# In the second block's weight stream, GpSimd instead of VectorE subtracts the rounded half of each tile

## The chip, the cores and the metric

The kernel runs on one core of one Trainium2 chip. The metric is the device time of one execution in microseconds (us), the median of several runs. Engines are named as the profile names them: PE is TensorE (PEld its weight loads), DVE is VectorE, ACT is ScalarE, POOL is GpSimd, SP is SyncE, whose queue issues nearly all DMAs.

## What is computed

Two transformer blocks run one after the other over 512 tokens of width 1024, all in fp32. The first block (four mixers, a gated merge, 32 experts) isn't touched by the change. The second block has two layers with these steps:

```python
h = rmsnorm(x, norm_pre[l])
(hq, hf_f, hf_b, hi, hz, ca, cb, cz, sb, sc, sv, sz,
 aq, ak, av, az, mq, mz) = split_cols(h @ w_in[l])
y_hg = hgrn2_branch(...)            # gated scan, forward and backward
y_cf = conformer_branch(...)        # depthwise convolution of 31 taps
y_sc = short_conv_branch(...)
y_at = window_attention(...) * jax.nn.silu(az)
mem_kv = rmsnorm(mem, mem_norm[l]) @ w_mem_kv[l]
y_mem = memory_cross_attention(mq, mem_kv) * jax.nn.silu(mz)
for n, yb in enumerate((y_hg, y_cf, y_sc, y_at, y_mem)):
    term = jax.nn.sigmoid(h @ w_gate[l, n]) * (yb @ w_branch[l, n])
    merged = term if merged is None else merged + term
x = x + rmsnorm(merged @ w_out[l], norm_post[l])
```

## The kernel before

**Split products.** A large product `W^T x` is made from rounded and residual halves in the format fp32r: `w_hi` is the tile rounded by ACT, `w_lo = w - w_hi` the rest, and the activations are kept as `x_hi` and `x_lo`. PE adds `w_hi*x_hi + w_hi*x_lo + w_lo*x_hi`, for each of eight slices of the contraction: 24 matmuls of 512 columns for one tile of 128 output channels (256 columns in `memory_keys`).

**The stream.** All weight tiles of a layer of the second block go through one `Stream`: 74 tiles a layer, 34 of projections (`w_in`) and 40 of the gates, and 8 tiles for both layers together in `memory_keys`, which runs once before the layers. That is 156 tiles in an execution. Raw tiles come in pairs into three slots `raw`; `w_hi` and `w_lo` have two buffers each. For tile n:

- ACT (`round`, L2053) waits until the raw pair is there and until PE has finished tile n-2 (`acc_done`), casts raw to `w_hi[n % 2]` and raises `rounded`.
- DVE (`rest`, L2077) waits for `rounded`, subtracts `w_hi` from raw into `w_lo[n % 2]` and raises `split`.
- PE (`pe`, L2111 to L2113) waits for `split` and runs the 24 matmuls into `acc[n % 2]`.
- ACT (`evict`, L2060 or L2064) copies `acc` out, or takes a tanh of it into `sg` where the tile is a gate.
- For a gate tile PE also runs two fp32 matmuls of the branch output (L2123, into `br`), after the previous gate tile's `mixed`, and DVE (`mix`, L2088 and L2094) multiplies them with `sg` and adds them to `merged`.
- SP (`load`) waits for `split` of the last tile of a raw slot before it loads the next pair into it.

Rounding and subtraction run one tile ahead of PE: `act` and `dve` of step n handle tile n+1, and evict or mix tile n-1.

**What sets the order.** Each engine has its program written out by hand, one stage after another; a stage is a block with a barrier at its end, and POOL begins every stage by clearing the semaphores of the one before (L171). Each layer has five stages that hold steps of the stream, and between the steps DVE does the stage's own work: `window_stage` (21 subtractions), `memory_stage` (8), `hgrn_stage` (12), `conv_stage` (18) and `merge_stage` (15). In `hgrn_stage` DVE computes scan arguments, scaled keys, masks and states in a written order with a stream step after each. In `conv_stage` the 31 taps of two channel tiles are 62 DVE instructions (L2797, L2799), five to a step, each of which adds `pad * w` to `conf`, the name `y_t` in the trace. DVE's `Chain` makes it wait for each of its own results.

```python
for s, n in enumerate(fill):
    stream.dve(dve, n)
    if s == 0:
        dve.wait_ge(blank, 2)
        dve.wait_ge(th_ready, 1)
        run(nc.vector.scalar_tensor_tensor(pad[:, :, H:H + S], th[:], 1.0, ca, ALU.add, ALU.mult))
    for tap in range(PER * s, min(PER * s + PER, 2 * TAPS)):
...
            run(nc.vector.scalar_tensor_tensor(conf[:, m, :], src, wt, conf[:, m, :], ALU.mult, ALU.add))
```

Of the kernel before, what the change touches and what calls it, by code (L numbers as in the profile page):

```python
# [15 lines left out]
F32 = mybir.dt.float32  # L16
# [1966 lines left out]
class Stream:  # L1983
# [87 lines left out]
        if n:  # L2071
            self.evict(act, n - 1)

    def rest(self, dve, n):
        if n < len(self.tiles):
            dve.wait_ge(self.rounded, n + 1)
            self.nc.vector.tensor_tensor(self.w_lo[:, n % 2], self.weights(n), self.w_hi[:, n % 2].bitcast(F32),  # L2077
                                         ALU.subtract).then_inc(self.split, 1)

    def mix(self, dve, n):  # L2080
# [11 lines left out]
        else:  # L2092
            dve.wait_ge(self.added, u)
            self.nc.vector.tensor_tensor(dst, dst, sg, ALU.add).then_inc(self.added, 1)  # L2094

    def dve(self, dve, n):
        if n == 0:
            self.rest(dve, 0)
        self.rest(dve, n + 1)
        if n:  # L2100
            self.mix(dve, n - 1)

# [153 lines left out]
def window_stage(c, stream, lead, fill, wj, k2, v, sink, y, strips):  # L2256
# [7 lines left out]
    with ExitStack() as ctx:  # L2264
# [4 lines left out]
        with c.stage() as block:  # L2269
            @block.sync  # L2270
            def _(sp):
# [9 lines left out]
                for s in range(steps):  # L2281
                    att.load_bias(sp, s + 2)
                    if s < len(fill):
                        stream.load(sp, fill[s] + 2)

            @block.tensor
            def _(pe):
                for n in lead:
                    stream.pe(pe, n)
                    if n == lead[3]:  # L2290
                        pe.wait_ge(stream.freed, lead[1] + 1)
                        for i in range(NT):
                            mm = pe.transpose(att.tps[:, 0, i * P:(i + 1) * P], vt[:, i * P:(i + 1) * P], c.const("ident"))
                        mm.then_inc(v_turned, 1)
                pe.wait_ge(k2_in, 64)
                pe.wait_ge(v_ready, 1)
                pe.wait_ge(stream.freed, lead[3] + 1)
                att.scores(pe, 0)
                for s in range(steps):
                    att.pe_step(pe, s)  # L2300
                    if s < len(fill):
                        stream.pe(pe, fill[s])
# [31 lines left out]
def memory_stage(c, stream, fill, qm, km, vm, y):  # L2334

    nc = c.nc
    gate = qm[:, 2:4]
    units = head_units(qm[:, 0:2], lambda h, b: km[b:b + 64, h // 2], lambda h, j: vm[:, j, h * HD:(h + 1) * HD],
                       y, 4, lambda i: (0, 2), None)
    with ExitStack() as ctx:  # L2340
        att = Attention(c, ctx, units, HD ** -0.5, gate)
        th = c.sb(ctx, "tanh", [P, 2, S])
        th_ready = c.sem("th")
        steps = len(units) + 2

        def beside(s):
            return [fill[s // 2]] if s % 2 == 0 and s // 2 < len(fill) else []

        with c.stage() as block:
            @block.sync  # L2350
            def _(sp):
                for n in fill:
                    stream.load(sp, n + 2)

            @block.tensor
            def _(pe):
                att.scores(pe, 0)
                for s in range(steps):
                    att.pe_step(pe, s)
                    for n in beside(s):  # L2360
                        stream.pe(pe, n)

            @block.scalar
            def _(act):
                nc.scalar.activation(th[:], gate, ACT.Tanh, scale=0.5).then_inc(th_ready, 1)
                for s in range(steps):
                    att.exps(act, s)
                    for n in beside(s):
                        stream.act(act, n)
                    att.turned(act, s - 1)  # L2370

            @block.vector
            def _(dve):
                att.run = Chain(dve, att.chain)
                for s in range(steps):
                    if s == 2:
                        dve.wait_ge(th_ready, 1)
                        att.run(nc.vector.scalar_tensor_tensor(gate, th[:], 1.0, gate, ALU.add, ALU.mult))
                    att.dve_step(dve, s)
                    for n in beside(s):  # L2380
                        stream.dve(dve, n)
# [73 lines left out]
def hgrn_stage(c, stream, fill, room, gate, lb, gain, y):  # L2455
# [6 lines left out]
    with ExitStack() as ctx:  # L2462
# [25 lines left out]
        with c.stage() as block:  # L2488
            @block.sync
            def _(sp):  # L2490
                for n in fill:
                    stream.load(sp, n + 2)

            @block.tensor
            def _(pe):
# [221 lines left out]
def conv_stage(c, stream, fill, glu, rest, w31, w3, bias, gain, shift, conf, short):  # L2717
# [6 lines left out]
    with ExitStack() as ctx:  # L2724
# [7 lines left out]
        with c.stage() as block:  # L2732
# [5 lines left out]
            @block.gpsimd  # L2738
            def _(pool):
                nc.gpsimd.memset(pad[:], 0.0).then_inc(blank, 1)  # L2740
                nc.gpsimd.memset(pad3[:], 0.0).then_inc(blank, 1)

            @block.tensor
            def _(pe):
# [116 lines left out]
def merge_stage(c, stream, fill):  # L2861

    with c.stage() as block:
        @block.sync
        def _(sp):
            for n in fill:
                stream.load(sp, n + 2)

        @block.tensor
        def _(pe):  # L2870
            for n in fill:
                stream.pe(pe, n)

        @block.scalar
        def _(act):
            for n in fill:
                stream.act(act, n)
            stream.evict(act, fill[-1])

        @block.vector  # L2880
        def _(dve):
            for n in fill:
                stream.dve(dve, n)
            stream.mix(dve, fill[-1])
# [244 lines left out]
```

## Time and profile before

| | |
|---|---|
| median of 3 runs | 3080.27 us (3079.12 to 3086.88) |
| the profiled execution, its own time | 3078.07 us |
| its span in the trace | 3076.3 us |
| PE busy | 2415.0 us, 79% |
| DVE busy | 1304.4 us, 42% |
| ACT busy | 739.3 us, 24% |
| POOL busy | 90.8 us, 3% |
| DMA queue of SP | 28.8% of 16 engines |
| mean granted TensorE clock | 0.85 |

The profile is one execution. Its span is 1.8 us shorter than that execution's time and its time 2.2 us under the median. "Idle before" is the time an engine stood before a group's instructions, with the instruction that released it. The second block runs from about 1608 us to the end: `memory_keys` to 1682 us, the first layer's stream from 1711 to 2298 us, the second's from 2407 to 2992 us. PE's records are pipelined: a matmul of 512 columns is shown with 0.39 us but the next starts 0.227 us later.

### The profile page before, as it was taken

What the parts mean: (1) busy time and instruction counts of PE and PEld (TensorE: products, weight loads), DVE (VectorE), ACT (ScalarE), POOL (GpSimd) and SP (SyncE); (2) the same over time, 40 slices, a digit from 0 to 9 for tenths busy, and PEclk for the clock granted to TensorE, in tenths of its full rate; (3) what the DMA queues carried; (4) which work ended last, traced back from release to release, by engine and by line L of the source; (5) the groups of instructions that cost most, each with busy time, mean ns of one, the idle gap of its engine ahead of it and who ended that gap; (6) DMA issues with size and microseconds to landing.
All of it is one profiled execution on the core that took longest, in us unless ns stands there. A gap on an engine that the chain in (4) does not pass through costs nothing. (4 is left out here: it accounts for less than half of the span.)

```text
span 3076.3 us, 30601 instructions
## 1 busy us (share of the span) xinstructions
PE 2415.0 (79%) x11062; PEld 1704.0 (55%) x11062; DVE 1304.4 (42%) x2309; ACT 739.3 (24%) x1285; POOL 90.8 (3%) x144
## 2 busy tenths in 40 slices
PE   5966457466998619999914799999985799999996
PEld 3833235355776514444404676677764676677764
DVE  1126843723333411111143345668533344668533
ACT  2222222201222101111103333322222333323221
POOL 0000000000000011111100000000000000000000
PEclk7965567556999759999966899999997899999997
DMA  4110100002221048777623432123311432123311
GB/s 151 36 71 22 31 30 20 11 7 104 102 102 55 16 118 302 267 265 266 224 97 111 125 109 49 52 69 100 117 55 60 132 102 65 52 69 96 115 53 73
DMA packets 264772, 300.05 MB, mean 98 GB/s; under 512 B 53667, under 2 KB 225779, under 8 KB 264630
## 3 DMA queue, kind: packets, MB, share of 16 engines
q1 hardware_dynamic: 255158, 289.78, 28.8%
q0 software_dynamic: 9472, 8.43, 0.8%
q8 instruction: 83, 1.36, 0.2%
q14 instruction: 59, 0.48, 0.1%
HBM read 289.13 MB, written 33.14 MB: 105 GB/s over the span
## 5 line engine op out<-in xcount | busy, mean ns | idle before, releaser
L2111 PE MATMUL acc<-x_hi,w_hi 128*128 128x512 f32 x1184 | 492.2, 416 | 16.5 <-DVE w_lo L2077 13.2
L2112 PE MATMUL acc<-x_lo,w_hi 128*128 128x512 f32 x1184 | 466.0, 394 | 0.0
L2113 PE MATMUL acc<-x_hi,w_lo 128*128 128x512 f32 x1184 | 465.9, 394 | 0.0
L2077 DVE TENSOR_TENSOR w_lo<-raw,w_hi 128x1024 fp32r<-128x1024 f32 x156 | 190.6, 1223 | 257.4 <-ACT w_hi L2053 254.3
L2053 ACT CAST w_hi<-raw 128x1024 fp32r<-128x1024 f32 x156 | 162.6, 1044 | 568.1 <-PE acc L2113 535.3
L2111 PEld LDWEIGHTS acc<-x_hi,w_hi 128*128 128x128 f32 x1184 | 225.9, 191 | 76.4 <-issue 18.2
L2112 PEld LDWEIGHTS acc<-x_lo,w_hi 128*128 128x128 f32 x1184 | 225.9, 191 | 54.7 <-issue 10.6
L1785 PE MATMUL ps<-wgu,xt 128*128 128x512 f32 x512 | 230.5, 603 | 30.6 <-ACT xt L1808 23.9
L2113 PEld LDWEIGHTS acc<-x_hi,w_lo 128*128 128x128 f32 x1184 | 225.1, 190 | 49.2
L1785 PEld LDWEIGHTS ps<-wgu,xt 128*128 128x128 f32 x512 | 95.6, 192 | 146.7 <-issue 118.4
L2123 PE MATMUL br<-y_t,raw_b 128*128 128x512 f32 x320 | 153.9, 604 | 7.2 <-DVE sg L2088 7.2
L1842 DVE TENSOR_TENSOR hid<-silu,ps 128x256 f32<-128x256 f32 x32 | 13.5, 421 | 273.2 <-ACT silu L1815 273.2
L1229 PE MATMUL ps<-x_hi,w_hi 128*128 128x512 f32 x256 | 113.9, 445 | 16.1 <-DVE w_lo L1290 16.1
L1775 PE MATMUL ps<-wd,hid_t 128*128 128x512 f32 x256 | 115.2, 593 | 0.9 <-DVE hid_t L1847 0.9
L360 PE MATMUL acc<-x_hi,w_hi 128*128 128x512 f32 x216 | 86.0, 398 | 25.8 <-DVE w_lo L349 25.8
L1328 PE MATMUL ps<-w_hi,m_hi 128*128 128x512 f32 x192 | 77.9, 405 | 34.5 <-DVE w_lo L1344 34.5
L1231 PE MATMUL ps<-x_hi,w_lo 128*128 128x512 f32 x256 | 100.9, 394 | 0.0
L1230 PE MATMUL ps<-x_lo,w_hi 128*128 128x512 f32 x256 | 100.5, 393 | 0.0
L2799 DVE SCALAR_TENSOR_TENSOR y_t<-pad,w,y_t 128x512 f32<-128x512 f32 x120 | 90.1, 751 | 3.4
L2123 PEld LDWEIGHTS br<-y_t,raw_b 128*128 128x128 f32 x320 | 60.7, 191 | 54.3 <-issue 48.3
L361 PE MATMUL acc<-x_lo,w_hi 128*128 128x512 f32 x216 | 85.3, 395 | 0.0
L362 PE MATMUL acc<-x_hi,w_lo 128*128 128x512 f32 x216 | 85.2, 395 | 0.0
(513 smaller groups left out, 3541.0 us busy)
## 6 DMA issues: line engine op xcount, KB each, us to landing
raw<-in_w_gate SPq DMA_DIRECT2D x40, 1024.0 KB, 5.2
raw<-in_w_in SPq DMA_DIRECT2D x34, 1024.0 KB, 5.5
wgu<-in_moe_w_gate SPq DMA_DIRECT2D x32, 1024.0 KB, 5.6
wgu<-in_moe_w_up SPq DMA_DIRECT2D x32, 1024.0 KB, 9.6
wd<-in_moe_w_down SPq DMA_DIRECT2D x32, 1024.0 KB, 11.5
wg<-in_w_in SPq DMA_DIRECT2D x8, 2048.0 KB, 7.7
y_t<-in_w_out SPq DMA_DIRECT2D x6, 2048.0 KB, 7.8
raw_b<-in_w_branch SPq DMA_DIRECT2D x40, 256.0 KB, 2.7
```

Source lines behind the costliest of these rows:

```text
L1229: pe.matmul(ps[:, m, :], hi, x_hi[:, k, :], start=(k == 0), stop=False)
L1230: pe.matmul(ps[:, m, :], hi, x_lo[:, k, :], start=False, stop=False)
L1231: pe.matmul(ps[:, m, :], lo, x_hi[:, k, :], start=False, stop=(k == KT - 1))
L1775: mm = pe.matmul(ps[:, 1 + 2 * u + half, :], ht[:, u, m * P:(m + 1) * P], wd[:, s % 4, m, half * 512:half * 512 + 512], start=(m == 0), st ...
L1785: mm = pe.matmul(ps[:, 0, :], xt[:, u, k, :], wgu[:, s, k, :], start=(k == 0), stop=(k == KT - 1))
L2053: self.nc.scalar.copy(self.w_hi[:, n % 2], self.weights(n)).then_inc(self.rounded, 1)
L2077: self.nc.vector.tensor_tensor(self.w_lo[:, n % 2], self.weights(n), self.w_hi[:, n % 2].bitcast(F32), ALU.subtract).then_inc(self.split, 1)
L2111: pe.matmul(acc, hi, tile.hi[:, k, :], start=(k == 0), stop=False)
L2112: pe.matmul(acc, hi, tile.lo[:, k, :], start=False, stop=False)
L2113: mm = pe.matmul(acc, lo, tile.hi[:, k, :], start=False, stop=(k == KT - 1))
L2123: mm = pe.matmul(self.br[:], self.raw_b[:, b % self.SLOTS, k, tile.half * P:(tile.half + 1) * P], tile.row[:, k, :], start=(k == 0), stop= ...
L2799: run(nc.vector.scalar_tensor_tensor(conf[:, m, :], src, wt, conf[:, m, :], ALU.mult, ALU.add))
```

## The change

The subtraction `rest` is issued by GpSimd instead of VectorE, with the same wait and the same semaphore. A new method `pool` issues it, one tile ahead as before, and every stage that holds stream steps gets a GpSimd program that does nothing else. In `conv_stage` it comes behind two memsets that GpSimd has there already. Nothing is changed for PE, ACT and SP.

```diff
-    def rest(self, dve, n):
+    def rest(self, pool, n):
         if n < len(self.tiles):
-            dve.wait_ge(self.rounded, n + 1)
-            self.nc.vector.tensor_tensor(self.w_lo[:, n % 2], self.weights(n), self.w_hi[:, n % 2].bitcast(F32),
+            pool.wait_ge(self.rounded, n + 1)
+            self.nc.gpsimd.tensor_tensor(self.w_lo[:, n % 2], self.weights(n), self.w_hi[:, n % 2].bitcast(F32),
                                          ALU.subtract).then_inc(self.split, 1)
...
+    def pool(self, pool, n):
+        if n == 0:
+            self.rest(pool, 0)
+        self.rest(pool, n + 1)
+
     def dve(self, dve, n):
-        if n == 0:
-            self.rest(dve, 0)
-        self.rest(dve, n + 1)
         if n:
             self.mix(dve, n - 1)
...
             def _(pool):
                 nc.gpsimd.memset(pad[:], 0.0).then_inc(blank, 1)
                 nc.gpsimd.memset(pad3[:], 0.0).then_inc(blank, 1)
+                for n in fill:
+                    stream.pool(pool, n)
```

The other four stages get a GpSimd program of the same loop (`for n in [*lead, *fill]` in `window_stage`, `for n in fill` elsewhere).

Below is POOL's order from the semaphore clears before `hgrn_stage` to `merge_stage`, the change against the kernel before. `ISA` at L171 is a clear of one semaphore, a branch enters a stage's program, and lines after L2077 have moved down by the inserted ones.

```order
 L171 ISA x13
+L2506 UNCONDITIONAL_BRANCH
+L2077 TENSOR_TENSOR w_lo<-raw,w_hi 128x1024 x12
 L167 UNCONDITIONAL_BRANCH
 L168 UNCONDITIONAL_BRANCH
 L171 ISA x27
-L2738 UNCONDITIONAL_BRANCH
-L2740 MEMSET pad 128x1084
-L2741 MEMSET pad_676 128x1028
+L2755 UNCONDITIONAL_BRANCH
+L2757 MEMSET pad 128x1084
+L2758 MEMSET pad_676 128x1028
+L2077 TENSOR_TENSOR w_lo<-raw,w_hi 128x1024 x18
```

POOL has nothing in `hgrn_stage` before, and 12 subtractions now; in `conv_stage` 18 subtractions stand behind the 27 clears and the two memsets.

DVE in `hgrn_stage`, before, from the subtraction behind `states(0)` to `scaled(1)`, whose products PE transposes next:

```order
L2077 TENSOR_TENSOR w_lo<-raw,w_hi 128x1024
L2088 SCALAR_TENSOR_TENSOR sg<-sg,br 128x512
L2094 TENSOR_TENSOR merged<-merged,sg 128x512
L2612 TENSOR_TENSOR_SCAN cum<-consts,g 128x512 x2
...
L2624 TENSOR_TENSOR ke<-end,cum 128x1024
L2077 TENSOR_TENSOR w_lo<-raw,w_hi 128x1024
L2088 SCALAR_TENSOR_TENSOR sg<-sg,br 128x512
L2094 TENSOR_TENSOR merged<-merged,sg 128x512
L2667 COPY y_t<-ps 128x4x64 x4
L2669 TENSOR_TENSOR y_t<-y_t,ps 128x2x448
L2630 TENSOR_TENSOR ke<-room,ke 128x1024
```

and the same stretch in the change:

```order
L2088 SCALAR_TENSOR_TENSOR sg<-sg,br 128x512
L2094 TENSOR_TENSOR merged<-merged,sg 128x512
L2629 SCALAR_TENSOR_TENSOR cum<-consts,g 128x512 x2
...
L2641 TENSOR_TENSOR ke<-end,cum 128x1024
L2088 SCALAR_TENSOR_TENSOR sg<-sg,br 128x512
L2094 TENSOR_TENSOR merged<-merged,sg 128x512
L2684 COPY y_t<-ps 128x4x64 x4
L2686 TENSOR_TENSOR y_t<-y_t,ps 128x2x448
L2647 TENSOR_TENSOR ke<-room,ke 128x1024
```

Two subtractions are gone from in front of `ke`; the rest stands as it stood.

DVE in `conv_stage`, before, in the middle of the taps:

```order
L2799 SCALAR_TENSOR_TENSOR y_t<-pad,w_551,y_t 128x512 x5
L2077 TENSOR_TENSOR w_lo<-raw,w_hi 128x1024
L2799 SCALAR_TENSOR_TENSOR y_t<-pad,w_551,y_t 128x512 x5
L2802 SCALAR_TENSOR_TENSOR rest<-tanh,rest 128x1024
L2077 TENSOR_TENSOR w_lo<-raw,w_hi 128x1024
```

and in the change, where the taps follow each other with nothing between:

```order
L2816 TENSOR_SCALAR y_t<-pad,w_551,conf_b 128x512 x2
L2818 SCALAR_TENSOR_TENSOR y_t<-pad,w_551,y_t 128x512 x33
```

## Rows read from the trace of the kernel before

**Rows 1.** Waits of PE, 1705 to 2300 us (first layer): total us, times, longest us.
```profile
PE acc L2111 <- DVE w_lo L2077: 6.9, 1, 6.9
PE br L2123 <- DVE sg L2088: 4.4, 2, 3.8
PE t_ps L2171 <- DVE probs_n L2219: 2.9, 7, 0.7
PE ps L2502 <- DVE ke L2630: 2.9, 1, 2.9
...
PE ps L2512 <- DVE rel L2633: 0.8, 1, 0.8
```

**Rows 2.** The same, 2405 to 3000 us (second layer).
```profile
PE br L2123 <- DVE sg L2088: 2.8, 2, 2.2
...
PE ps L2512 <- DVE rel L2633: 2.0, 2, 1.2
```

**Rows 3.** The page's costliest groups: busy us, mean ns, idle before, releaser.
```profile
L2077 DVE TENSOR_TENSOR w_lo<-raw,w_hi 128x1024 fp32r<-128x1024 f32 x156 | 190.6, 1223 | 257.4 <-ACT w_hi L2053 254.3
L2053 ACT CAST w_hi<-raw 128x1024 fp32r<-128x1024 f32 x156 | 162.6, 1044 | 568.1 <-PE acc L2113 535.3
```

**Rows 4.** Timeline, one tile of window_stage: start us, us, engine, line, operation.
```profile
1722.14 1.05 ACT L2053 CAST w_hi<-raw 128x1024 fp32r<-128x1024 f32 x1 [8.60 <-PE acc L2113]
...
1723.22 1.23 DVE L2077 TENSOR_TENSOR w_lo<-raw,w_hi 128x1024 fp32r<-128x1024 f32 x1 [8.24 <-ACT w_hi L2053]
...
1727.32 0.39 PE L2111 MATMUL acc<-x_hi,w_hi 128*128 128x512 f32 x1
```

**Rows 5.** Timeline, one tile of memory_keys.
```profile
1663.77 1.23 DVE L2077 TENSOR_TENSOR w_lo<-raw,w_hi 128x1024 fp32r<-128x1024 f32 x1 [1.66 <-ACT w_hi L2053]
...
1665.32 0.28 PE L2111 MATMUL acc<-mem_hi,w_hi 128*128 128x256 f32 x1
```

**Rows 6.** Groups of POOL: its smallest instruction that reads SBUF.
```profile
L1715 POOL COPY gi<-table 128x1 uint32 (+1 forms) x32 | 6.4, 199 | 24.5 <-PE ps L1765 16.3 <-DVE xg L1825 8.2
```

**Rows 7.** Timeline, hgrn_stage, DVE and then ACT.
```profile
1955.01 1.23 DVE L2677 TENSOR_SCALAR room<-g 128x2048 f32<-128x2048 f32 x1
...
1987.14 1.23 DVE L2077 TENSOR_TENSOR w_lo<-raw,w_hi 128x1024 fp32r<-128x1024 f32 x1
...
1998.43 1.23 DVE L2077 TENSOR_TENSOR w_lo<-raw,w_hi 128x1024 fp32r<-128x1024 f32 x1
...
2003.96 1.23 DVE L2630 TENSOR_TENSOR ke<-room,ke 128x1024 f32<-128x1024 f32 x1
...
1989.61 1.04 ACT L2053 CAST w_hi<-raw 128x1024 fp32r<-128x1024 f32 x1 [8.48 <-PE acc L2113]
...
2002.43 1.03 ACT L2053 CAST w_hi<-raw 128x1024 fp32r<-128x1024 f32 x1
```

**Rows 8.** Timeline, conv_stage, POOL, DVE and then PE.
```profile
2066.40 0.95 POOL L2741 MEMSET pad<- 128x1028 f32 x1
...
2067.80 1.23 DVE L2791 SCALAR_TENSOR_TENSOR pad<-tanh,glu 128x1024 f32<-128x1024 f32 x1 [1.64 <-ACT tanh L2761]
...
2094.15 3.90 DVE L2799 SCALAR_TENSOR_TENSOR y_t<-pad,w,y_t 128x512 f32<-128x512 f32 x5
...
2126.41 0.68 DVE L2088 SCALAR_TENSOR_TENSOR sg<-sg,br 128x512 f32<-128x512 f32 x1
...
2069.47 0.39 PE L2111 MATMUL acc<-x_hi,w_hi 128*128 128x512 f32 x1
...
2131.08 1.88 PE L2123 MATMUL br<-y_t,raw_b 128*128 128x512 f32 x4
```

**Rows 9.** Windows, a tile behind a stage change and the next: us, busy, PEclk, DMA.
```profile
1860.80:1868.60 7.80, 7.80 (x26) 6.13 (x25) 4.69 (x10) 2.62 (x6) 0.00 (x0) 0.68 0.54 4
1873.10:1878.50 5.40, 5.40 (x26) 4.49 (x27) 3.67 (x9) 2.28 (x5) 0.00 (x0) 1.00 0.37 127
```

More of the change, by code:

```diff
@@ L2284, in _ @@
                         stream.load(sp, fill[s] + 2)
+            @block.gpsimd
+            def _(pool):
+                for n in [*lead, *fill]:
+                    stream.pool(pool, n)
             @block.tensor
@@ L2353, in _ @@
                     stream.load(sp, n + 2)
+            @block.gpsimd
+            def _(pool):
+                for n in fill:
+                    stream.pool(pool, n)
             @block.tensor
@@ L2492, in _ @@
                     stream.load(sp, n + 2)
+            @block.gpsimd
+            def _(pool):
+                for n in fill:
+                    stream.pool(pool, n)
             @block.tensor
@@ L2741, in _ @@
                 nc.gpsimd.memset(pad3[:], 0.0).then_inc(blank, 1)
+                for n in fill:
+                    stream.pool(pool, n)
             @block.tensor
@@ L2867, in _ @@
                 stream.load(sp, n + 2)
+        @block.gpsimd
+        def _(pool):
+            for n in fill:
+                stream.pool(pool, n)
         @block.tensor
```

## Prediction

> **What bounds the kernel now.** I read the waits of PE first. In the first layer's stream of some 590 us PE waits for DVE in few places [rows 1]: 6.9 us for the layer's first `w_lo`, 4.4 us in two waits of the branch product for `sg`, 2.9 us for `ke`, 0.8 us for `rel`, and seven times 0.4 us for `probs_n` in `memory_stage`, a chain of small instructions with no subtraction ahead of it. The second layer shows `sg` and `rel` with 2.8 and 2.0 us [rows 2] and the row for `ke` again, word for word. These three, 8.1 and 7.7 us, lie in `hgrn_stage`. Everywhere else PE has work, so the stream is bound by PE, and a DVE that gets lighter helps in `hgrn_stage` alone.
>
> Then the groups. DVE spends 190.6 us on 156 subtractions of 1.22 us [rows 3]; this is what leaves DVE. ACT stood 535 of its 568 us of idle time before `w_hi` because PE had not finished the tile two back, not for a DMA. So the raw tiles come early, and loads that SP issues one us later (it waits for `split`) stay hidden under that margin.
>
> Then one tile of the steady stream [rows 4]. The cast ends at 1723.19 us, DVE subtracts to 1724.45, PE takes the tile at 1727.32: 2.87 us to spare, so a subtraction of up to 4.1 us costs PE nothing here. PE's time for a tile is 24 times 0.227, 5.44 us. In `memory_keys`, with 256 columns, the margin is 1665.32 - 1665.00 = 0.32 us [rows 5].
>
> **The price of one subtraction on POOL.** The trace has no two-input instruction on POOL. Below: its memset of 1028 columns takes 0.95 us, and it reads nothing [rows 8]. Above: two reads and a write in turn, three such passes, plus the 0.2 us of a POOL copy of one element [rows 6], 3.05 us. Two passes with the write beside them and the 0.2 give 2.1 us. I take X = 2.3 us, nearer to two passes than to three; both ends stay for the range.
>
> The Trainium skill, GPSIMD Engine Reference, section 3.1 (elementwise), gives 4497 ns for a two-input add over 2048 fp32 columns, as an estimate 2.25 us for 1024. No row here shows it. By it the sum would be some 2 us lower.
>
> **The change part by part.**
> - *First tiles.* The first tile of `memory_keys` and of each layer is waited for in full [rows 1]. Three times X - 1.22 = 1.08: **+3.2 us**.
> - *memory_keys.* Tiles 2 to 7 have 0.32 us to spare: six times 1.08 - 0.32 = 0.76: **+4.5 us**.
> - *Start of `conv_stage`.* POOL clears 27 semaphores and does two memsets before its first subtraction, which can start at 2067.35 [rows 8] and ends at 2069.65. PE wants that tile at 2069.47: 0.2 us late, **+0.4 us** for both layers. Other stages begin with 4 to 17 clears, hidden behind the cast and the tile made ahead.
> - *All other tiles.* X is under 4.1 us: nothing. PE covers it; the cost beyond it would be X - 4.1 a tile.
> - *`hgrn_stage`, DVE's side.* The first `sg` wait has one subtraction of 1.14 us (start to start) right ahead of it; the second `sg` wait, `ke` and `rel` have two (at 1987.14 and 1998.43, with `ke` from 2003.96) [rows 7]; the second layer's first `rel` wait another 0.8. With nothing in exchange: 1.2 + 2.4 in the first layer, 1.2 + 0.8 + 2.4 in the second, **-8.0 us**.
> - *Everything else that DVE sheds* (taps, attention, merges) lies beside a busy PE: nothing.
>
> Without any effect of the two engines on each other this is +8.1 - 8.0, nothing.
>
> **What the two engines do to each other** is the unknown that decides. DVE passes 2048 columns of one input (`room<-g`) in 1.23 us [rows 7], and the subtraction reads two inputs of 1024 columns in the same 1.23: both draw 2048 columns. So DVE seems to have two read streams and the two-input instruction needs both, while POOL now reads two tiles of its own. Either POOL has a path of its own (price 0) or it takes one of DVE's (price up to X for each subtraction that meets a two-input DVE instruction). No row shows a large read of POOL beside DVE. I take the second end, since no row shows a third stream.
>
> The Trainium skill, SBUF — State Buffer, section "Who interferes with whom", says that DVE and GpSimd share a port pair under an exclusive lock, that a DVE instruction with two SBUF inputs contends with a GpSimd instruction that reads SBUF, and that the later one blocks until the other ends. By this rule the change loses; by ports of their own it breaks even. The trace neither confirms nor denies it.
>
> - *`conv_stage` with the price.* A tile's step on DVE is five taps, 3.9 us [rows 8]. With a subtraction of its own, 1.14 from start to start, it is 5.04 us, under PE's 5.44. With X of standing still it is 6.2 us: **DVE becomes the bound.** PE needs the first `mix`, behind 55 taps, at 2131.08 for its branch product; before it was there at 2127.1. Now from 2067.80: two 1024-column instructions 2 x 1.4, 55 taps of 0.78 = 42.9, the mix 0.7, that is 2114.2; the first subtraction of POOL holds DVE X - 0.45, eleven more hold it X each: 2113.75 + 12 X. Against 2131.08 PE waits 12 X - 17.3 = 10.3 us. Point of break-even: X = 1.44 us. Behind such a stand PE's clock is lower for a while: behind a stage change the granted clock was 0.68, between its levels 1.2 and 2.4 GHz, and 26 matmuls took 7.8 where they take 5.4 us at 1.00 [rows 9]; I put 2 us. **+24.6 us** for two layers.
> - *`hgrn_stage` with the price.* Casts end at 1990.65 and 2003.46 [rows 7], inside DVE's run of two-input instructions in front of `ke` and `rel`; one more does so in the first half. Three holds of X against four subtractions of 1.14: 3 X - 4.6 = 2.3 us a layer, **+4.6 us** in place of -8.0.
>
> **Sum:** 3.2 + 4.5 + 0.4 + 24.6 + 4.6 = 37.3 us on the profiled execution's 3078.07: 3115.4. That execution lies 2.2 us under the median of the three runs, so I forecast **3118 us**. With X = 1.9 the same sum is 3100, with 2.75 it is 3138, with 3.05 about 3150; with 0.95 it is under 3078.
>
> **Rivals.**
> - *No interference (not slower).* DVE's taps stay at 0.78 us apart and POOL works beside them. Place: `conv_stage` and `hgrn_stage`. For it: the two engines have instruction streams of their own and PE hides a slower subtraction; against: the count of read streams. 3078.07 + 8.1 - 8.0 + 2.2 = **3080 us**, 3076 with X = 1.9 and 3088 with 3.05. It decides once a two-input DVE instruction beside POOL lasts as long as alone. Chance 0.35.
> - *Partial interference.* DVE loses a part of X, up to half, under the break-even of 1.44 us: only the 8 us of small terms and a little in `hgrn_stage`. Around 3085 to 3100. Chance 0.09.
> - *POOL too slow.* X over 4.1 us: PE waits on most of the 156 tiles, each X - 4.1, and at 5 us that is beyond 3180. Three passes are 3.05, so it needs a conversion to fp32r at a cost that no row shows. Chance 0.04.
> - That POOL is the one that gets held (it loses to DVE's next tap each time) is no case of its own: taps and subtraction still add up to 6.2 us a tile.
>
> **How the numbers follow.** Forecast 0.52, rivals 0.35, 0.09 and 0.04. A measurement of this kernel can tell about 0.3%, 9 us, from no change: under 3071 is faster, over 3089.5 slower. Slower: 0.52 + 0.04 + 0.06 = 0.62. Same: 0.33, nearly all of it the first rival. Faster 0.05: no case that I worked out gets there, only one with X near 1 us and gains in clock. The likeliest case's own range is 3100 to 3138; as the first rival must be let in, the range is 3077 to 3138, which leaves out the lowest tail of that rival and X over 2.75.
>
> **What would show it.** POOL's group L2077: 156 times, mean about 2.3 us, POOL busy near 450 us where it was 91. DVE's taps (now L2818): instructions of 0.75 us beside POOL either stay or reach up to 3 us, or start late with POOL as the reason; the group's mean or the idle time before it would grow by some 25 us a layer. PE's wait for `sg` in `conv_stage` about 10 us once a layer, the taps' end near 84 instead of 70 us after their start. In `memory_keys` tiles 3.6 instead of 2.9 us apart. If taps keep their pace, the forecast is wrong; if POOL's mean is under 1.5 us, too.

## The result and the profile after

| | median, us | runs | ratio to before |
|---|---|---|---|
| before | 3082.25 (3079.12 to 3086.88) | 4 | |
| changed | 3121.62 (3120.12 to 3129.36) | 4 | 1.0132 [1.0109, 1.0154] |

The change makes the kernel 39 us, 1.3%, slower. The forecast was 3118 us.

The profiled execution of the changed kernel took 3129.36 us with a span of 3127.6, 51.3 us more than that of before. Not all of this is the change. Here is the first cast of `memory_keys`, where the changed region begins, in the timeline of before:

```profile
1645.85 1.99 ACT L2053 CAST w_hi<-raw 128x1024 fp32r<-128x1024 f32 x2 [0.86 <-PEq L167]
```

and of the changed kernel, with the first subtractions on POOL and PE's start behind them:

```profile
1659.18 1.99 ACT L2053 CAST w_hi<-raw 128x1024 fp32r<-128x1024 f32 x2 [0.75 <-PEq L167]
1660.31 4.67 POOL L2077 TENSOR_TENSOR w_lo<-raw,w_hi 128x1024 fp32r<-128x1024 f32 x2 [91.97 <-ACT w_hi L2053]
...
1662.70 0.58 PE L2113 MATMUL acc<-mem_hi,w_hi 128*128 128x256 f32 x1 [4.68 <-POOL w_lo L2077]
```

The two profiled executions differ by 13.3 us before that cast, where the program is the same. From the cast to the end it is 1430.4 us before and 1468.4 after, **38.0 us more**, which agrees with the medians. Single executions differ like this ahead of that cast (it began at 1646.1 and 1657.9 us in two of the runs below), so I compare stretches from here on and set the medians beside them.

The page's engines and its groups that answer to [rows 3]:

```profile
PE 2429.2 (78%) x11062; PEld 1711.1 (55%) x11062; DVE 1262.1 (40%) x2153; ACT 739.2 (24%) x1285; POOL 473.4 (15%) x300
...
L2077 POOL TENSOR_TENSOR w_lo<-raw,w_hi 128x1024 fp32r<-128x1024 f32 x156 | 382.4, 2452 | 1068.8 <-ACT w_hi L2053 1068.8
...
L2053 ACT CAST w_hi<-raw 128x1024 fp32r<-128x1024 f32 x156 | 162.6, 1044 | 615.5 <-PE acc L2115 582.5
...
L2818 DVE SCALAR_TENSOR_TENSOR y_t<-pad,w,y_t 128x512 f32<-128x512 f32 x120 | 134.6, 1121 | 4.3
```

POOL is 382.6 us busier, and DVE, which gave away 190.6 us, is only 42.3 us lighter: 148 us have come back to it without one instruction more. The 120 taps show where a part of them went: 134.6 us in place of 90 (60 of 751 ns a layer, below).

The same part of `conv_stage` in the first layer, all taps, with shortest, median and longest in ns; first before, then after:

```profile
L2799 DVE SCALAR_TENSOR_TENSOR y_t<-pad,w,y_t x60: 743/752/755, 2070.3 to 2135.7; 128x512 f32<-128x512 f32 x60
```

```profile
L2818 DVE SCALAR_TENSOR_TENSOR y_t<-pad,w,y_t x60: 742/752/2879, 2092.7 to 2165.4; 128x512 f32<-128x512 f32 x60
```

The median stands still at 752 ns, and the longest is 2.1 us longer than any of before. An average of 1121 ns would suggest that every tap is slower; the three numbers say that most keep their pace and a few stand still. Sixty taps take 67.3 us in place of 45.1, and 22.2 / 2.0 is 11: one tap for each of the subtractions that fall among them. The rest that came back lies in the additions and copies into `merged` (49 us over all 80), in attention's maximum with its sink (17 us) and in scans and products, most of it beside a busy PE.

Waits of PE, 1960 to 2070 us (`hgrn_stage`, first layer) in the changed kernel, against [rows 1]:

```profile
PE br L2125 <- DVE sg L2088: 6.0, 3, 5.2
PE ps L2529 <- DVE rel L2650: 4.8, 2, 3.1
PE ps L2519 <- DVE ke L2647: 2.9, 1, 2.9
```

then 2060 to 2200 us (`conv_stage`), where PE waited for nothing of DVE before:

```profile
PE br L2125 <- DVE sg L2088: 8.4, 1, 8.4
PE acc L2113 <- PEq L167: 0.5, 1, 0.5
PE acc L2113 <- POOL w_lo L2077: 0.4, 1, 0.4
```

and 1655 to 1690 us (`memory_keys`):

```profile
PE acc L2113 <- POOL w_lo L2077: 7.0, 4, 4.7
```

In `hgrn_stage` the three rows are 13.7 us against 8.1 before, 5.6 us more, and the stage has grown by 5.6.

The stretches of the stream, from the timelines, in us: `memory_keys` from the first cast to its last matmul; `hgrn_stage` from DVE's first instruction there (`om`) to that of `conv_stage` (`half`); `conv_stage` from there to PE's first matmul of the next stage's first tile; the last column from the first cast to the end of the span.

| | memory_keys | hgrn 1, 2 | conv 1, 2 | to the end |
|---|---|---|---|---|
| before | 28.0 | 114.4, 113.6 | 119.6, 119.6 | 1430.4 |
| changed | 31.4 | 119.9, 118.7 | 132.0, 131.2 | 1468.4 |

`merge_stage` has 113.4 us in both kernels and both layers. The remaining column, `window_stage` with `memory_stage`, has 237.9 and 236.7 us before, 234.0 and 239.3 after: it moves by 3 to 4 us in either direction with PE's granted clock, which is 0.96 and 0.97 before, 0.99 and 0.96 after. The same happens without any change: in e3_pool_conv below, where this part is as before, it took 237.8 us at 0.96 in the first layer and 232.7 at 0.99 in the second. The times of `hgrn_stage` and `conv_stage` repeat within 1 us where nothing is changed in them; a sum over a whole execution is good to a few.

### The profile page after: what moved, and what is told of

It is laid out like the page before. It is cut to its first block and busy times, and to the rows that moved or that the text cites. A ratio compares the mean times of both kernels' runs of the same rounds, so it can differ in the third digit from the quotient of the medians.

```text
span 3127.6 us, 30571 instructions
## 1 busy us (share of the span) xinstructions
PE 2429.2 (78%) x11062; PEld 1711.1 (55%) x11062; DVE 1262.1 (40%) x2153; ACT 739.2 (24%) x1285; POOL 473.4 (15%) x300
## 5 line engine op out<-in xcount | busy, mean ns | idle before, releaser
L2077 POOL TENSOR_TENSOR w_lo<-raw,w_hi 128x1024 fp32r<-128x1024 f32 x156 | 382.4, 2452 | 1068.8 <-ACT w_hi L2053 1068.8
L2115 PE MATMUL acc<-x_hi,w_lo 128*128 128x512 f32 x1184 | 466.0, 394 | 0.0
L2114 PE MATMUL acc<-x_lo,w_hi 128*128 128x512 f32 x1184 | 465.4, 393 | 0.0
L1662 POOL DMA_INDIRECT table<-entries,slots x8 | 7.9, 989 | 1132.5 <-DMA table<-table 1130.3
L2088 DVE SCALAR_TENSOR_TENSOR sg<-sg,br 128x512 f32<-128x512 f32 x80 | 55.0, 687 | 201.6 <-PE br L2125 162.2
L2818 DVE SCALAR_TENSOR_TENSOR y_t<-pad,w,y_t 128x512 f32<-128x512 f32 x120 | 134.6, 1121 | 4.3
## 6 DMA issues: line engine op xcount, KB each, us to landing
wd<-in_moe_w_down SPq DMA_DIRECT2D x32, 1024.0 KB, 11.6
```

What stands on the lines that cost most here:

```text
L2077: self.nc.gpsimd.tensor_tensor(self.w_lo[:, n % 2], self.weights(n), self.w_hi[:, n % 2].bitcast(F32), ALU.subtract).then_inc(self.split, 1)
L2114: pe.matmul(acc, hi, tile.lo[:, k, :], start=False, stop=False)
L2115: mm = pe.matmul(acc, lo, tile.hi[:, k, :], start=False, stop=(k == KT - 1))
```

## The experiments

The theory: a DVE instruction with two inputs in SBUF and a POOL instruction that reads SBUF can't run together; one stands still until the other is done. The rivals: POOL's slower subtraction itself is what is late (places beside DVE don't matter), or POOL's writes are what DVE meets.

### Where the loss sits: POOL in some stages only

Three kernels give POOL only the tiles of a set, DVE the others; at a change of engine the subtraction waits for the one ahead.

```diff
+    def on_pool(self, n):
+        return False if self.merged is None else n in ON_POOL
...
-    def rest(self, pool, n):
-        if n < len(self.tiles):
-            pool.wait_ge(self.rounded, n + 1)
-            self.nc.gpsimd.tensor_tensor(self.w_lo[:, n % 2], self.weights(n), self.w_hi[:, n % 2].bitcast(F32),
-                                         ALU.subtract).then_inc(self.split, 1)
+    def rest(self, on, eng, n, mine):
+        if n < len(self.tiles) and self.on_pool(n) == mine:
+            if n and self.on_pool(n - 1) != mine:
+                on.wait_ge(self.split, n)
+            on.wait_ge(self.rounded, n + 1)
+            eng.tensor_tensor(self.w_lo[:, n % 2], self.weights(n), self.w_hi[:, n % 2].bitcast(F32),
+                              ALU.subtract).then_inc(self.split, 1)
```

**e1_pool_heavy**: `ON_POOL` is tiles 29 to 58 of a layer, `hgrn_stage` and `conv_stage`.

> GpSimd subtracts only for the tiles of hgrn_stage and conv_stage (30 of a layer's 74), DVE for all others. Theory 'hold' (a GpSimd instruction that reads SBUF holds DVE's SBUF instructions until it ends): nearly all of the 39 us are there, conv_stage 2 x 12.4 and hgrn_stage 2 x 5.6, so about 3118 us. Theory 'late' (the tile comes 1.2 us later and PE waits for it, on any tile): 30/74 of the loss, about 3098 us.

**e2_pool_light**: all the others, with `memory_keys`.

> The complement: GpSimd subtracts in memory_keys, window_stage, memory_stage and merge_stage, DVE in hgrn_stage and conv_stage. 'Hold': memory_keys 3.4 us and 1.2 us for each layer's first tile, about 3088 us; no wait of PE in conv_stage. 'Late': the rest of the loss, about 3105 us.

**e3_pool_conv**: tiles 41 to 58, `conv_stage` alone.

> GpSimd subtracts only for the 18 tiles of conv_stage. 'Hold': 2 x 12.4 us, about 3107 us, with PE's one wait of some 8.4 us for sg in each layer. 'Late': 18/74, about 3092 us.

| | median, us | ratio to before | memory_keys | hgrn 1, 2 | conv 1, 2 | to the end |
|---|---|---|---|---|---|---|
| e1_pool_heavy | 3114.80 | 1.0115 [1.0086, 1.0144] | 26.7 | 118.2, 119.2 | 131.3, 131.8 | 1458.7 |
| e2_pool_light | 3088.79 | 1.0031 [1.0016, 1.0046] | 31.6 | 114.3, 114.7 | 119.6, 119.6 | 1437.0 |
| e3_pool_conv | 3102.46 | 1.0075 [1.0046, 1.0104] | 27.9 | 114.4, 114.1 | 131.5, 131.4 | 1451.1 |

Before had 3080.68 us beside these (15 runs). The 96 subtractions of e2 cost 8 us in all and the 60 of e1 34 us; the 36 of `conv_stage` alone cost 22. So it isn't the length of POOL's instruction that counts but how much DVE has to do beside it before PE wants the result: additions into `merged` are held in `merge_stage` too, with no wait of PE for them. (The last column is one execution for each kernel; that of e1 was the fastest of its four, 3106.9 us.) The loss stays in its stage: with POOL in `conv_stage` alone the conv column is that of the changed kernel and the hgrn column that of before.

### Taps that read one input from SBUF

**e7_taps_psum** is the changed kernel with 60 of the 62 taps of a layer reading a zeroed tile in PSUM in place of `pad`; the convolution is left out by this, the number and size of the instructions are the same.

```diff
-                    run(nc.vector.scalar_tensor_tensor(conf[:, m, :], src, wt, conf[:, m, :], ALU.mult, ALU.add))
+                    run(nc.vector.scalar_tensor_tensor(conf[:, m, :], ps[:, 2, :], wt, conf[:, m, :], ALU.mult, ALU.add))
```

> The changed kernel, but the 60 multiply-add taps of a layer read PSUM (a zeroed bank) instead of pad, so each has one SBUF tensor input; the convolution is left out by this. 'Hold', if it takes two SBUF inputs: the taps keep about 0.7 us beside GpSimd, conv_stage loses nothing, about 3122 - 25 = 3097 us. If any DVE instruction is held, or in theory 'late': no change, about 3122 us.

Median 3100.46 us, ratio 1.0069 [1.0046, 1.0091]. The taps in the same view:

```profile
L2819 DVE SCALAR_TENSOR_TENSOR y_t<-ps,w,y_t x60: 735/751/754, 2089.6 to 2152.2; 128x512 f32<-128x512 f32 x60
```

POOL's subtractions are all still there (156 of 2416 ns in the mean), and no tap is longer than alone. `conv_stage` is back at 120.3 and 120.1 us while `hgrn_stage` keeps its 119.9 and 119.6. This is the sharpest of the runs: besides one memset a layer that zeroes the bank, nothing was changed but where one of the two inputs comes from, and 11 to 12 us a layer went. From the first cast to the end it is 1444.3 us, 24 less than the changed kernel; the medians, taken in two sets of runs, differ by 21.

The changed kernel itself has the same test without any edit. Its `sg` products read one input from PSUM and one from SBUF, 52 of the 80 began while a POOL subtraction ran, and none is longer than 0.69 us. The additions into `merged` right behind them read both inputs from SBUF and take up to 1.94:

```profile
L2088 DVE SCALAR_TENSOR_TENSOR sg<-sg,br x80: 674/687/690, 1887.4 to 3043.9; 128x512 f32<-128x512 f32 x80
L2094 DVE TENSOR_TENSOR merged<-merged,sg x64: 691/1596/1936, 1983.3 to 3044.6; 128x512 f32<-128x512 f32 x64
```

### Which POOL work holds DVE: writes, one read, two reads

Three kernels leave the subtraction on DVE and add idle work on POOL in `conv_stage` only, behind the same wait, for the first 12 tiles.

```diff
+                own = Chain(pool, beside)
+                for n in fill[:12]:
+                    pool.wait_ge(stream.rounded, n + 2)
+                    for _ in range(3):
+                        own(nc.gpsimd.memset(idle[:, 0:820], 0.0))
```

**e4_extra_write** is this. **e5_extra_read2** has in place of the memsets one `tensor_tensor(idle[:], c.consts[:, 0:1024], c.consts[:, 870:1894], ALU.subtract)`, and **e6_extra_read1** two copies `tensor_copy(idle[:], c.consts[:, 0:1024])`.

> The kernel before (DVE subtracts), with idle work on GpSimd in conv_stage: for each of its first 12 tiles, when the tile is rounded, three memsets of 820 columns into a scratch tile, some 2.3 us, nothing waits for them. It only writes SBUF. 'Hold by reads': nothing, 3081 us, taps stay at 0.75 us. 'Hold by any GpSimd instruction': DVE gets 12 x 2.3 us more to do, its spare 4 us gone, PE waits over 20 us a layer, about 3125 us.

> The same place, but the idle work is one subtraction of two 1024-column pieces of the constants into the scratch tile, about 2.35 us. No product waits for it, so theory 'late' expects no change, 3081 us. 'Hold': 12 x 2.3 us on DVE beside its own subtractions, less 4 us to spare, 22 to 24 us a layer, about 3127 us.

> The same place, the idle work is two copies of 1024 columns of the constants, one input each; their length is not known, 1 to 1.5 us each. If any GpSimd read of SBUF holds DVE: 12 x (2 to 3) less 4 us a layer, 3120 to 3145 us. If only a two-input GpSimd instruction holds it: 3081 us.

| | median, us | ratio to before | conv 1, 2 | to the end |
|---|---|---|---|---|
| e4_extra_write | 3080.78 | 1.0011 [0.9991, 1.0031] | 119.6, 119.6 | 1430.5 |
| e5_extra_read2 | 3107.88 | 1.0105 [1.0077, 1.0134] | 135.0, 134.9 | 1458.5 |
| e6_extra_read1 | 3110.41 | 1.0115 [1.0086, 1.0143] | 131.7, 131.6 | 1450.9 |

(Before beside them 3078.47 us, 13 runs.) Taps and POOL's work in `conv_stage` of e4, by groups of 2050 to 2190 us (busy us, mean ns, idle before):

```profile
L2805 DVE SCALAR_TENSOR_TENSOR y_t<-pad,w,y_t 128x512 f32<-128x512 f32 x60 | 45.0, 751 | 1.7
```

```profile
L2747 POOL MEMSET idle<- 128x820 f32 x36 | 28.3, 786 | 32.2 <-ACT w_hi L2053 30.8
```

of e5:

```profile
L2804 DVE SCALAR_TENSOR_TENSOR y_t<-pad,w,y_t 128x512 f32<-128x512 f32 x60 | 61.7, 1028 | 1.7
```

```profile
L2746 POOL TENSOR_TENSOR idle<-consts 128x1024 f32<-128x1024 f32 x12 | 26.7, 2229 | 47.4 <-ACT w_hi L2053 47.3
```

and of e6:

```profile
L2805 DVE SCALAR_TENSOR_TENSOR y_t<-pad,w,y_t 128x512 f32<-128x512 f32 x60 | 60.4, 1007 | 1.7
```

```profile
L2747 POOL COPY idle<-consts 128x1024 f32<-128x1024 f32 x24 | 31.0, 1290 | 40.7 <-ACT w_hi L2053 39.9
```

All three keep POOL busy for about the same 27 to 31 us. Writes alone cost the taps nothing. Reads hold them, with one input as with two: 22 copies held 22 taps by 15.4 us in sum, and ten subtractions ten taps by 16.7. For e5 I had expected 3127 us, from twelve holds of 2.3 us less 4 to spare. All twelve subtractions do hold an instruction in the first layer, ten a tap and two the instructions ahead of these taps, but by 1.6 us each, 19.6 in sum: they are shorter than the real ones (2.2 us in the mean), and a part of each lies beside an instruction of DVE (see the pieces below). 19.6 less 4 is 15.6, and the stage grew by 15.4. PE meets it elsewhere than in the changed kernel: DVE's own `w_lo` stands in the held queue, and PE waited 8.8 us in seven waits for it and 1.1 for `sg`; in e6 it is 7.1 and 0.7. In e6, 24 copies hold 16.3 us in sum, less 4 is 12.3, and the stage grew by 12.1. Its median stands 2.5 us over that of e5 all the same, and its profiled execution, with 3098.2 us, was the fastest of four, so I go by the stage.

### Pieces: does the hold end with the instruction?

**e8_pieces** is the changed kernel with the subtraction in four instructions of 256 columns, **e11_halves** with two of 512; only the last raises `split`.

```diff
+            for k in range(0, KT, 2):
+                ins = self.nc.gpsimd.tensor_tensor(self.w_lo[:, n % 2, k:k + 2], self.weights(n)[:, k:k + 2],
+                                                   self.w_hi[:, n % 2, k:k + 2].bitcast(F32), ALU.subtract)
+            ins.then_inc(self.split, 1)
```

> The changed kernel with each GpSimd subtraction cut into four of 256 columns. If the hold lasts one instruction, taps get in between the pieces: no tap lasts more than 0.75 + 0.7 us, and a tile's four pieces stretch over up to 4 x (0.65 + 0.78) = 5.7 us, past the 4.1 us that PE leaves, so that PE waits on w_lo in conv_stage too; the four starts add 0.2 us each. About 3130 us. If DVE is held for a sum of the same length without gaps: 3122 us and four times the small holds.

> The changed kernel with each subtraction in two instructions of 512 columns on GpSimd; it stands between one piece (taps 1121 ns in the mean, conv_stage 132 us, whole 3122 us) and four (1011 ns, 124 us, 3101 us). Theory: a held VectorE instruction loses what is left of the one GpSimd instruction that it met, and the two engines take turns instruction by instruction; a start or an end of each piece, 0.1 to 0.2 us, lies beside a tap and costs nothing, so more pieces cost less. Then two pieces lie between: taps 1060 to 1100 ns, conv_stage 127 to 130 us, whole 3108 to 3116 us. Rival: the gain of four pieces comes from their size alone (a tap of 512 columns is longer than a piece of 256 and wins every turn), with nothing gained at a piece as long as a tap: taps 1110 to 1130 ns, conv_stage 131 to 132 us, whole 3120 us.

| pieces | median, us | ratio to before | taps, mean ns | conv 1, 2 | hgrn 1, 2 | to the end |
|---|---|---|---|---|---|---|
| 1 (changed) | 3121.62 | 1.0132 [1.0109, 1.0154] | 1122 | 132.0, 131.2 | 119.9, 118.7 | 1468.4 |
| 2 (e11) | 3114.01 | 1.0102 [1.0073, 1.0131] | 1072 | 128.3, 127.9 | 119.0, 118.3 | 1462.7 |
| 4 (e8) | 3101.16 | 1.0079 [1.0051, 1.0106] | 1011 | 124.2, 124.2 | 117.9, 117.2 | 1457.6 |

For e8 I had no gain in view, and it gained 20 us; e11 came out inside the ranges of its theory and not where the rival put it. The tap view of e11 and then of e8:

```profile
L2820 DVE SCALAR_TENSOR_TENSOR y_t<-pad,w,y_t x60: 740/752/1790, 2091.4 to 2162.5; 128x512 f32<-128x512 f32 x60
```

```profile
L2820 DVE SCALAR_TENSOR_TENSOR y_t<-pad,w,y_t x60: 750/1108/1227, 2081.3 to 2150.6; 128x512 f32<-128x512 f32 x60
```

and POOL's group of e8 from 2050 to 2190 us (in `memory_keys` eight pieces take 5.5 to 5.7 us), then PE's wait for it from 2040 on:

```profile
L2078 POOL TENSOR_TENSOR w_lo<-raw,w_hi 128x256 fp32r<-128x256 f32 x84 | 80.7, 990 | 54.7 <-ACT w_hi L2053 54.7
```

```profile
PE acc L2115 <- POOL w_lo L2078: 2.9, 4, 1.9
```

A tap is held at most 2.1 us by one piece of 1024 columns, 1.04 by one of 512 and 0.48 by one of 256: the hold ends with the POOL instruction that was met, and the next tap gets in before the next piece. In turn POOL waits: a piece of 256 takes 0.99 us in the mean, against 0.73 where DVE stands idle. The taps of one layer were held 22.2, 19.2 and 15.6 us in sum. A subtraction in four pieces holds less in all, because a part of every piece lies beside a tap. Piece by piece: 11, 21 and 43 taps were held by 2.03, 0.92 and 0.36 us in the mean, and a piece takes 2.39, 1.29 and 0.73 us where DVE does nothing, so each holds 0.36 to 0.37 us less than it lasts, whatever its size. At the end of a hold 0.20 us of this can be seen: every held tap of the three kernels lost what was left of POOL's instruction when the tap began, less 0.20 us. Four pieces save the 0.37 four times and are 0.54 us longer in all than one. This is worked out from the rows; why it is 0.37 stays open. The price of pieces is where PE waits for `w_lo`: from a layer's first cast to its first matmul it is 3.52, 3.66 and 3.94 us, and 2.9 of the 4.6 us that `conv_stage` still loses in e8 are the row above.

### A version that uses the rule

**e9_best** starts from the kernel before. POOL takes only tiles 32 and 35 of a layer, both in `hgrn_stage`, whose rounding ends while DVE is idle or works on inputs in PSUM, and DVE does the gate work of three tiles ahead of its own subtractions. **e10_order** has the second part alone.

```diff
-    def rest(self, dve, n):
-        if n < len(self.tiles):
+    def rest(self, dve, n, pool=False):
+        on_pool = self.merged is not None and n in (32, 35)
+        if n < len(self.tiles) and on_pool == pool:
+            if self.merged is not None and n in (32, 33, 35, 36):
+                dve.wait_ge(self.split, n)
...
+            @block.gpsimd
+            def _(pool):
+                for n in (32, 35):
+                    stream.rest(pool, n, True)
...
-                stream.dve(dve, U[0])
+                stream.mix(dve, U[0] - 1)
+                stream.rest(dve, U[0] + 1)
                 dve.wait_ge(f_ready, 2)
                 arguments(0)
-                stream.dve(dve, U[1])
+                stream.mix(dve, U[1] - 1)
                 scaled(0)
+                stream.rest(dve, U[1] + 1)
```

> The kernel before, with GpSimd subtracting only two tiles a layer, 32 and 35, both in hgrn_stage, whose rounding ends where VectorE waits or works on instructions with one input in PSUM; and at the head of that stage the gate work of three tiles is put ahead of VectorE's own subtractions. If a subtraction on GpSimd costs nothing where VectorE does not read SBUF alone beside it, the stage loses 3.4 to 4 us of TensorE's waits a layer: hgrn_stage 114.3 -> about 111 us, the whole 7 us under the kernel before, 3075 us where before has 3082. If each of the two subtractions holds VectorE all the same (2 us each, four in all, on the path), the gain is eaten: 3080 to 3085 us, with hgrn_stage at 113 to 115 us.

> The same order on VectorE at the head of hgrn_stage as e9_best, with no work on GpSimd at all. If the gain of e9_best lies in the order alone, this one has the same stage time within 1 us. If the two subtractions that leave VectorE matter, their 2.4 us of VectorE time (1.2 us each) come back in front of the gate work and this one is 1 to 2 us a layer slower than e9_best: hgrn_stage 112 to 113 us, the whole 3077 to 3079 us where before has 3082.

| | median, us | ratio to before | hgrn 1, 2 |
|---|---|---|---|
| e9_best | 3073.04 (12 runs) | 0.9973 [0.9958, 0.9989] | 112.5, 111.2 |
| e10_order | 3080.21 (12 runs) | 0.9986 [0.9970, 1.0002] | 113.6, 113.4 |

Before beside them 3080.35 us (23 runs). The timeline of e9, POOL and then DVE around its second instruction:

```profile
2021.05 2.36 POOL L2080 TENSOR_TENSOR w_lo<-raw,w_hi 128x1024 fp32r<-128x1024 f32 x1 [33.69 <-ACT w_hi L2053]
```

```profile
2015.99 1.22 DVE L2653 TENSOR_TENSOR cum<-room,cum 128x1024 f32<-128x1024 f32 x1
2022.99 0.48 DVE L2659 COPY state<-ps 128x64 f32<-128x64 f32 x2 [5.78 <-PE ps L2529]
2023.51 3.76 DVE L2662 SCALAR_TENSOR_TENSOR state<-state,dec,ps 128x64 f32<-128x64 f32 x12
```

The subtraction lies in DVE's idle 5.8 us, and the copy and the state steps beside and behind it, which read PSUM, keep the 0.48 and 3.76 us that they have elsewhere. The other three subtractions on POOL lie in the same way; all four take 2.35 to 2.36 us, and no DVE instruction beside them is longer than alone. So these four cost DVE nothing, which is what the run shows firmly.

What the version gains is less sure. The whole is 0.27% under before: the interval leaves out 1, but it is within the 0.3% that I had called the bound. The traces don't settle it. e9 is 4.3 us shorter in `hgrn_stage` over both layers than before and e10 1.0, but PE's waits there are 15.1 us in e9, 17.6 in e10 and 15.7 before. Of the 3.3 us between e9 and e10, 2.6 are waits; of the 4.3 against before, 0.7 are waits and 3.5 are PE's own busy time, which was shorter at a granted clock of 0.97 in both layers where before had 0.94 and 0.95. From the first cast to the end e9 and e10 had the same, 1423.8 and 1424.1 us, against 1430.4: e10 got its part in the second layer's `window_stage` with `memory_stage`, 232.9 us in place of 236.7, where its program is that of before. And e10 missed its forecast for the stage, 112 to 113 us, by half a microsecond.

## Why the prediction was right

The sign, the mechanism and the size of the sum held: forecast +37.3 us on the profiled execution, measured +38.0 from the first cast on, a closeness that is in part luck (last point). By its own steps:

- **X, one subtraction on POOL.** Taken 2.3 us. Shortest, median and longest of the changed kernel are 2.34, 2.40 and 3.16:

```profile
L2077 POOL TENSOR_TENSOR w_lo<-raw,w_hi x156: 2336/2397/3163, 1660.3 to 3028.9; 128x1024 fp32r<-128x1024 f32 x156
```

  The estimate from the Trainium skill (GPSIMD Engine Reference, section 3.1), 2.25 us by halving its 4497 ns for 2048 columns, is a little under all of them.
- **First tiles, +3.2.** From first cast to first matmul 2.36 us before, 3.52 after, three times: +3.5.
- **memory_keys, +4.5.** Measured 3.36 - 1.16 = 2.2 us. I charged 0.76 to each of six tiles. The row above has four waits, one of 4.7 us for the first tile and three of 0.77 for tiles 2, 4 and 6. Tiles 3 to 7 do have 0.31 to 0.32 us to spare before. What was wrong is that each was charged by itself: the cast of tile n+1 waits for PE's end of tile n-1 and not of the late tile n, so when tile n comes late, tile n+1 has that time more (0.11 to 0.13 us to spare, no wait).
- **Start of conv_stage, +0.4.** A wait of 0.4 us in the first layer and 0.2 in the second: +0.6.
- **All other tiles, nothing.** No wait for `w_lo` elsewhere, with 2.87 us to spare.
- **conv_stage with the price, +24.6.** Measured +12.4 and +11.6, that is 24.0, of which 0.6 is the point above. Two parts of it were off in opposite ways and all but cancelled, which is luck. The wait for `sg` is 8.4 us in both layers, not 10.3: the holds, 11 taps by 2.0 us each and the two instructions ahead of them, come to 26.1 us and not 12 X - 0.45 = 27.2. The remaining 0.8 us of this I have not traced. And PE's clock behind the stand costs more than the 2 us that I put:

```profile
2158.80:2166.80 8.00, 7.96 (x19) 5.00 (x20) 7.60 (x11) 0.00 (x0) 0.00 (x0) 0.62 0.35 114
2170.00:2178.00 8.00, 8.00 (x28) 4.94 (x27) 3.51 (x5) 0.87 (x2) 2.35 (x1) 1.00 0.00 0
```

  (windows of the changed kernel, columns as in [rows 9]). Right behind the 8.4 us in which PE had nothing the granted clock was 0.62, a mean between its two levels, 1.2 and 2.4 GHz, and ten microseconds later 1.00. The stage grew by 12.4 us and the waits by 8.8, which leaves 3.6. PE's busy time in the stage fits this: 121.8 us at a granted clock of 0.96, against 118.4 at 1.00 before. In the second layer it is 121.2 us at 0.96, and 3.0 are left.
- **hgrn_stage with the price, +4.6: the mis-sized term.** Measured +5.6 and +5.0, 10.6 us. I counted three holds of two-input instructions against four subtractions saved. The trace has six holds in the first layer, five of them ahead of PE's last wait for DVE there. DVE's timeline of the changed kernel:

```profile
1965.90 4.40 DVE L2693 TENSOR_SCALAR g<-g,om,lb 128x512 f32<-128x512 f32 x4 [3.26 <-ACT g L2602]
...
1974.21 4.44 DVE L2629 TENSOR_TENSOR_SCAN cum<-consts,g 128x512 f32<-128x512 f32 x2
...
1988.75 1.93 DVE L2094 TENSOR_TENSOR merged<-merged,sg 128x512 f32<-128x512 f32 x1
...
2006.81 2.14 DVE L2630 COPY end<-cum 128x16 f32<-128x16 f32 x1
...
2020.67 3.37 DVE L2649 TENSOR_TENSOR ex<-room,ex 128x1024 f32<-128x1024 f32 x1
```

  The same in the kernel before (`merged` and `ex` from the first half):

```profile
1952.68 2.30 DVE L2676 TENSOR_SCALAR g<-g,om,lb 128x512 f32<-128x512 f32 x4 [2.90 <-ACT g L2585]
...
1959.96 2.48 DVE L2612 TENSOR_TENSOR_SCAN cum<-consts,g 128x512 f32<-128x512 f32 x2
...
1969.85 1.22 DVE L2632 TENSOR_TENSOR ex<-room,ex 128x1024 f32<-128x1024 f32 x1
...
1973.97 0.69 DVE L2094 TENSOR_TENSOR merged<-merged,sg 128x512 f32<-128x512 f32 x1
...
1992.12 0.18 DVE L2613 COPY end<-cum 128x16 f32<-128x16 f32 x1
```

  They are held by 2.1, 2.0, 1.2, 2.0 and 2.1 us, 9.4 in sum, against 4 x 1.14 = 4.6 saved: 4.8 of the layer's 5.6. (The sixth, a product into `y_t`, is 1.25 us longer near the stage's end, and PE does not wait behind it.) Two of the five, `g` and `end`, have one input: my count looked for two-input instructions only. So the first wait for `sg`, from which I took a subtraction off, grew from 3.8 to 5.2 us. The step that failed is "three holds of X". Two smaller slips stand in the range: by its own terms the sum is 3102 us with X = 1.9 and 3136 with 2.75, not 3100 and 3138, which changes nothing here.
- **The rest, nothing.** e2, with POOL everywhere but in the two stages above, is 6.6 us longer from the first cast on, and `memory_keys` and the layers' first tiles are 5.9 of it. In the changed kernel the parts above add up to 40.3 us, so the rest gave 2.3 back, mostly through the granted clock in `window_stage` and `memory_stage`. That the sum, 37.3, comes so close to 38.0 is luck: `memory_keys` was put 2.3 us too high and `hgrn_stage` 6.0 too low, and the clock gave the rest.

The rival *no interference* (3080 us) fell with the first row of the taps. Its argument, instruction streams of their own and a PE that hides a slower subtraction, is true and was not the point: e7 is that rival brought about in `conv_stage`, and there it holds. *Partial interference* fell as well for whole subtractions, since a held tap loses what is left of POOL's instruction but for 0.20 us. My sentence that a POOL held by DVE makes "no case of its own" was wrong for pieces: e8 and e11 show that finer turns cost less than the sum.

The rule of the Trainium skill (SBUF — State Buffer, section "Who interferes with whom"), a lock that the later of a two-input DVE instruction and a reading GpSimd instruction waits for, is borne out by the rows of e4 to e8, the 2.1 us above all. The same section of the Trainium skill says that an instruction with one SBUF input is free of it outside of modes that take both ports. The taps of e7 agree, with one input in PSUM. So do the instructions with one input, once their pace is known. In the kernel before, a DVE copy from SBUF takes 0.43 us for 512 columns and 0.69 for 1024, while a reduction takes 0.55 for 384 and 1.22 for 1024: 128 columns more cost the copy 0.07 us and the reduction 0.13, so the copy takes two columns in the time in which the reduction takes one. In the changed kernel copies are held (`merged<-sg`), and reductions are not, though 26 of the 64 lay wholly beside a subtraction of POOL:

```profile
L2091 DVE COPY merged<-sg x16: 427/1516/1523, 1888.2 to 2690.0; 128x512 f32<-128x512 f32 x16
L2207 DVE TENSOR_REDUCE stat<-scores x64: 419/420/554, 1767.7 to 2670.8; 128x1 f32<-128x256 f32 x48, 128x1 f32<-128x384 f32 x16
```

`g` is of the copies' kind: its 0.55 us for 512 columns is less than the reduction's pace would allow (0.69 us for 512 in the first block), and 0.12 over the 0.43 of a scaling by constants there.

## What to carry to other kernels

Before work goes to GpSimd to relieve VectorE, ask what VectorE does in that moment, not how busy either is: beside instructions with two inputs in SBUF, and beside copies and scalings from SBUF to SBUF, a GpSimd instruction that reads SBUF is added to VectorE's time, and one that VectorE did in 1.2 us came back as 2.0. In these runs such work cost VectorE nothing where it waited, read one of its inputs from PSUM or made a reduction, and writes of GpSimd cost its two-input instructions nothing. If it must overlap, pieces hold less than the whole (15.6 us in four, 22.2 in one), but try them where nobody waits for the result. And in a group's row look at shortest, median and longest rather than at the mean.

## What the runs showed of the hardware beyond the forecast

- One-input copies and scalings from SBUF to SBUF are held like two-input instructions: `end<-cum`, 16 columns, 2.14 in place of 0.18 us, `merged<-sg` 1.52 in place of 0.43. Reductions of one input are not, nor are instructions with one of two inputs in PSUM.
- A copy on POOL with one input (1.29 us for 1024 columns in the mean) holds a tap by 0.70 us in the mean, a subtraction of e5 by 1.6; three memsets of 820 columns hold no two-input tap. But in each layer of e4 one of the two `TENSOR_SCALAR` taps, the kind that takes two columns at a time, took 861 ns beside them where it has 546 alone, so writes are not free for every form.
- It works both ways: POOL's subtraction takes 2.34 to 2.40 us where DVE does nothing and up to 3.16 beside it, and four pieces that take 2.9 us alone were stretched to 4.0 in `conv_stage` (84 pieces of 0.99 us).

What stays open: why each POOL instruction holds 0.37 us less than it lasts, and whether e9 is faster than before by more than its clock.
